# Second-key one-hots of the last quads on GpSimd, and the first v gathers issued between them

## The reference, cut to what matters

```
u_sel = u[expert]                      # 256 tokens x 128 chosen rows
v_sel = v[expert]
act = gelu(einsum('td,thkd->thk', x, u_sel))
out = einsum('thk,thkd->td', gate * act, v_sel)
h = layer_norm(ALPHA * h + out, ln2_g, ln2_b)
```

## Time and profile before

| | |
|---|---|
| median of 3 runs | 2725.31 us (2724.09 to 2729.93) |
| span of the profiled execution, first to last instruction | 2723.7 us |
| time around that span | not shown on its own; the lowest run is 0.4 us longer than the span, the median 1.6 us |
| TensorE busy | 2335.6 us, 86% |
| VectorE busy | 1951.1 us, 72% |
| GpSimd busy | 2045.3 us, 75% |
| ScalarE busy | 1283.7 us, 47% |
| TensorE's mean granted clock | 0.916 |

### The profile page before, as it was taken

How to read it: one execution, slowest core, us unless ns; L and a number is a source line. 1 busy time by engine, 2 the same in 40 slices (tenths; PEclk the granted TensorE clock), 3 DMA queues, 4 the chain that set the end, 5 groups by cost and what they waited for, 6 DMA issues and landing times. The chain is left out here.

```text
span 2723.7 us, 41417 instructions
## 1 busy us (share of the span) xinstructions
PE 2335.6 (86%) x13836; PEld 2071.9 (76%) x13836; DVE 1951.1 (72%) x2992; ACT 1283.7 (47%) x2249; POOL 2045.3 (75%) x1052
## 2 busy tenths in 40 slices
PE   7998999999999999999999876773334479999996
PEld 6997888888888888999988766772322368888885
DVE  4999752633514417456525999989998899999998
ACT  5435555455454455343433012327996844444442
POOL 4776888888888887778783566778788847777773
PEclk9999999999999999999999988885556589999998
DMA  6553465565555654554455999999999969999996
GB/s 218 171 162 113 170 179 176 192 187 187 185 187 185 185 186 161 173 198 166 148 187 186 413 391 384 378 422 417 379 416 384 395 219 384 385 365 374 380 371 256
DMA packets 232086, 722.75 MB, mean 265 GB/s; under 512 B 17388, under 2 KB 53796, under 8 KB 198816
## 3 DMA queue, kind: packets, MB, share of 16 engines
q1 hardware_dynamic: 168480, 355.69, 38.6%
q0 software_dynamic: 57344, 360.74, 33.1%
q10 hardware_dynamic: 6144, 4.81, 0.6%
HBM read 717.51 MB, written 3.67 MB: 265 GB/s over the span
## 5 line engine op out<-in xcount | busy, mean ns | idle before, releaser
L460 POOL TENSOR_TENSOR w_lo<-raw,w_hi 128x1024 fp32r<-128x1024 f32 x464 | 1131.2, 2456 | 293.0 <-ACT w_hi L1161 291.1
L1161 ACT CAST w_hi<-raw 128x1024 fp32r<-128x1024 f32 x464 | 483.6, 1050 | 634.7 <-PE bank L598 406.6
L596 PE MATMUL bank<-B,w_hi 128*128 128x512 f32 x1280 | 454.7, 400 | 11.3 <-DVE B L1746 7.0
L596 PE MATMUL bank<-A,w_hi 128*128 128x512 f32 x1280 | 451.2, 398 | 1.6 <-DVE A L1759 1.6
L598 PE MATMUL bank<-B,w_lo 128*128 128x256 f32 x1280 | 359.8, 281 | 0.0
L598 PE MATMUL bank<-A,w_lo 128*128 128x256 f32 x1280 | 358.4, 280 | 0.0
L1879 DVE TENSOR_TENSOR sq<-bank,T 128x256 f32<-128x256 f32 x128 | 54.1, 424 | 409.8 <-ACT T L1342 409.7
L601 PE MATMUL bank<-A,w_hi 128*128 128x256 f32 x1152 | 330.7, 287 | 6.7 <-DVE upad L1823 5.3
L550 POOL DMA_INDIRECT vrows<-in_peer_v,ering x192 | 265.3, 1382 | 87.6 <-DVE rest L2294 43.4
L602 PE MATMUL bank<-A,w_hi 128*128 128x256 f32 x1152 | 326.6, 283 | 0.0
L603 PE MATMUL bank<-A,w_lo 128*128 128x256 f32 x1152 | 326.5, 283 | 0.0
(11 more groups left out here) (348 smaller groups left out, 5187.4 us busy)
## 6 DMA issues: line engine op xcount, KB each, us to landing
raw<-in_mlp_w SPq DMA_DIRECT2D x128, 1024.0 KB, 5.2
v_raw<-in_peer_v SPq DMA_DIRECT2D x128, 672.0 KB
raw<-in_w_in SPq DMA_DIRECT2D x40, 1024.0 KB, 4.9
raw<-in_cc_w_in SPq DMA_DIRECT2D x64, 512.0 KB, 5.0
raw<-in_cc_w_out SPq DMA_DIRECT2D x16, 1024.0 KB, 5.0
raw<-in_w_out SPq DMA_DIRECT2D x16, 1024.0 KB, 5.0
raw<-in_peer_wq SPq DMA_DIRECT2D x8, 1024.0 KB, 11.2
wq_t<-in_peer_wq SPq DMA_DIRECT2D x2, 2048.0 KB, 24.4
```

The lines of the kernel that those rows point to most:

```text
L460: nc.gpsimd.tensor_tensor(w_lo[:, s % 4], raw[:, s // 2, 2 * (s % 2):2 * (s % 2) + 2, :], w_hi[:, s % 4].bitcast(F32), ALU.subtract).then_ ...
L596: nc.tensor.matmul(bank[m][:].rearrange("p (s t) -> p s t", s=2), wh, both[:, :, kt, :], start=(kt == 0), stop=False)
L1161: nc.scalar.copy(w_hi[:, s % 4], raw[:, s // 2, 2 * (s % 2):2 * (s % 2) + 2, :]).then_inc(hi_done, 1)
```

## The change

For 12 of the last 16 quads (q modulo 4 below 3: 48, 49, 50, 52, 53, 54, 56, 57, 58, 60, 61, 62) GpSimd makes the second key's one-hots, with four tensor_scalar instructions of 128 x 128 a quad, and raises a new semaphore `key_hot_ok`. VectorE makes for those only the four products, and for quads 51, 55, 59 and 63 all five instructions as before. GpSimd does its first two quads ahead of the wait for the last dot product, then the expert copy, and then in turns one of the six gathers and one quad, until the gathers are used up; the last four quads follow without gathers. Each quad waits on GpSimd for its buffer (`quad_ps`). TensorE waits for both semaphores. Loops over the last 16 quads on TensorE and VectorE become straight-line code.

```
+LAST_QUADS = range(EARLY_STEPS, TOK // 4)
+POOL_QUADS = [q for q in LAST_QUADS if q % 4 < 3]
+def key_hots(q):
+    return 4 * sum(p <= q for p in POOL_QUADS)
+def vector_hots(q):
+    return 13 * EARLY_STEPS + sum(4 + (p not in POOL_QUADS) for p in LAST_QUADS if p <= q)
@@ gpsimd
+            def key_hot(q):
+                pool.wait_ge(keyT_ok, 1)
+                pool.wait_ge(quad_ps, q + 1)
+                for i in range(4):
+                    nc.gpsimd.tensor_scalar(hot[:, q % 2, 1, i, :], cst[:, C_IOTA:C_IOTA + KEYS],
+                                            keyT[:, 1, 4 * (q - 32) + i:4 * (q - 32) + i + 1], None, ALU.is_equal
+                                            ).then_inc(key_hot_ok, 1)
             V_FIRST = NT * SLOTS // RING
+            for q in POOL_QUADS[:2]:
+                key_hot(q)
             pool.wait_ge(row_used, RING + NT * SLOTS)
             value_experts(0, 0, 0)
-            value_rows(V_FIRST, 0, 0, V_ROWS)
+            for n, q in enumerate(POOL_QUADS[2:]):
+                if n < V_ROWS:
+                    value_rows(V_FIRST, 0, n, 1)
+                key_hot(q)
@@ tensor
+            def quad(q, h):
+                pe.wait_ge(mat_ok, q + 1)
+                for i in range(4):
+                    last = nc.tensor.matmul(misc[2 + h][:, i * P:(i + 1) * P], hot[:, h, 1, i, :],
+                                            hot[:, h, 0, i, :], start=True, stop=True)
+                last.then_inc(quad_ps, 1)
+            def last_quads(first, end):
+                for q in range(first, end):
+                    pe.wait_ge(oh_ok, vector_hots(q))
+                    pe.wait_ge(key_hot_ok, key_hots(q))
+                    quad(q, q % 2)
-            quads(24, 1)
+            last_quads(48, 50)
             part_weights(3)
             pe.wait_ge(coefT_ok, 1 + PARTS)
-            quads(25, 7)
+            last_quads(50, 64)
@@ vector
-            def one_hots(r):
-                for h in range(2):
-                    q = 2 * r + (h + 32)
-                    dve.wait_ge(quad_ps, q + 1)
+            def one_hots(q):
+                h, first = q % 2, 4 * (q - 32)
+                dve.wait_ge(quad_ps, q + 1)
+                if q not in POOL_QUADS:
                     V.tensor_tensor(hot[:, h, 1], iota.unsqueeze(1).broadcast_to([P, 4, KEYS]),
...
+            for q in LAST_QUADS[:2]:
+                one_hots(q)
             part_coefficients(3)
+            for q in LAST_QUADS[2:8]:
+                one_hots(q)
             dve.wait_ge(coefT_ok, 1 + PARTS)
+            for q in LAST_QUADS[8:]:
+                one_hots(q)
```

More of the change, by code:

```diff
@@ L313, in build @@
             "keyT_ps", "keyT_ok", "coefT_ps", "coefT_ok", "oh_ok", "quad_ps", "mat_ok")
-        key_neg_ok = sem("key_neg_ok")
+        key_neg_ok, key_hot_ok = sems("key_neg_ok", "key_hot_ok")
         fq_ps, fq_ok, ln1_scaled = rbB_ok, n_out["rms1"], BT_in
@@ L1051, in quads @@
                     for h in range(2):
[L1052 to L1061, removed]
+                        pe.wait_ge(oh_ok, 13 * (2 * r + h) + 13)
+                        quad(2 * r + h, h)
+            def last_quads(first, end):
[3 more added lines that the diff above has]
+                    quad(q, q % 2)
             def row_turned(n):
@@ L2248, in gates_in_parts @@
                 dve.sem_inc(half_ok, 1)
-            def one_hots(r):
-                for h in range(2):
-                    q = 2 * r + (h + 32)
-                    dve.wait_ge(quad_ps, q + 1)
+            def one_hots(q):
+                h, first = q % 2, 4 * (q - 32)
+                dve.wait_ge(quad_ps, q + 1)
+                if q not in POOL_QUADS:
                     V.tensor_tensor(hot[:, h, 1], iota.unsqueeze(1).broadcast_to([P, 4, KEYS]),
[L2256 to L2262, removed]
+                                    keyT[:, 1, first:first + 4].unsqueeze(2).broadcast_to([P, 4, KEYS]), ALU.is_equal
+                                    ).then_inc(oh_ok, 1)
+                for i in range(4):
+                    V.tensor_scalar(hot[:, h, 0, i, :], iota, keyT[:, 0, first + i:first + i + 1],
+                                    coefT[:, 1, first + i:first + i + 1], ALU.is_equal, ALU.mult).then_inc(oh_ok, 1)
             def coefficients(t, n):
@@ L2345, in _ @@
             dve.wait_ge(coefT_ok, PARTS)
-            with dve.Fori(EARLY_STEPS // 2 - 16, EARLY_STEPS // 2 - 15) as r:
-                one_hots(r)
+            for q in LAST_QUADS[:2]:
+                one_hots(q)
             part_coefficients(3)
-            with dve.Fori(EARLY_STEPS // 2 - 15, EARLY_STEPS // 2 - 12) as r:
-                one_hots(r)
+            for q in LAST_QUADS[2:8]:
+                one_hots(q)
             dve.wait_ge(coefT_ok, 1 + PARTS)
-            with dve.Fori(EARLY_STEPS // 2 - 12, 16) as r:
-                one_hots(r)
+            for q in LAST_QUADS[8:]:
+                one_hots(q)
             dve.wait_ge(rest_ok, 1)
```

## The result

The changed kernel takes 2739.82 us in the median of six runs (2729.57 to 2745.70); six runs of the kernel before on the same chips took 2730.61 (2724.09 to 2733.79). The ratio is 1.005 with an interval of 1.0031 to 1.0068: slower by 9.2 us between the medians, and by 13.7 at the centre of the interval. The prediction was 2726.6 us, 1.3 later than before, with a range of 2721 to 2733. It was wrong: the time lies above the range. The range also ended 7.7 us above the 2725.3 from which it was reckoned, and the shift was 9.2.

What follows compares the result with a forecast made beforehand. VectorE paces the last quads before; after the change GpSimd is slowest from quad 52. With t = 0.36, 2206.9 + 32 t puts quad 63 at 2218.4, 1.3 us later: 2725.3 + 1.3 = 2726.6 us, range 2721 to 2733.

Steps and rivals of the forecast that it cites:

- The limit of what can be won: Quads 52 to 63: two-buffer round of 1.3 us a quad, plus quad 48's sooner start, allows at most 4.2 us.
- The price t: One GpSimd 128x128 tensor_scalar for the one-hots: taken as 0.36 us, 0.33 plus 0.03 for the port.
- The prediction's other estimate, 0.38: Same GpSimd tensor_scalar, from 1.8 cycles an element at 1.2 GHz: near 0.38 us, end 0.6 us later.
- The rest of the sum: GpSimd series from quad 52: one-hots, gathers 5.0, buffer wait 1.5, last steps 3.2; quad 63 starts at 2206.9 + 32 t.
- quad 62's own way: End of the GpSimd series: path through quad 62, claimed shorter than that through quad 61 while t is under 0.5.
- Before quad 50: First eight GpSimd one-hots beside VectorE's dots: 0.6 us delay against 0.61 saved, net 0; quad 50 at 2195.17 as before.
- signs that the prediction had named for being wrong: t under 0.3, one-hots of quads 48 and 49 unfinished when VectorE leaves the dots, or PEclk 0.5 in last quads.
- The fourth rival: Before quad 50: all 8 GpSimd instructions delay the dots in full, 4.4 us later, 2729.7 us; chance 0.07.
- The first (cheap instruction): GpSimd one-hots cost only 0.2 to 0.26 us each: 2721.1 to 2723.6 us; chance 0.18.
- The second (the lock at full length): Each GpSimd one-hot from 2197 waits out a VectorE product: t 0.585, 8.5 us later, 2733.8 us; chance 0.12.
- The third (the clock): TensorE half busy in last quads falls to 1.2 GHz: 2.1 us there, about 2 in dense, 2730.7 us; chance 0.11.

Runs made afterwards that it cites:

- both runs: Changed kernel with GpSimd copies for tensor_scalar: last dot product to first dense matmul 30.2 us; changed kernel with half the GpSimd one-hot instructions: 32.2 us.
- the run with the filler: Changed kernel plus four identity matmuls on TensorE ahead of each quad from 50 on: last dot product to first dense matmul 43.3 us, ratio 1.0014.
- first experiment: Kernel before plus 20 extra GpSimd instructions ahead of its first weight work: tensor_scalar 0.59 us each; last dot product to first dense matmul 31.5 us.

## Why the prediction was wrong, point by point

**The limit of what can be won** (4.2 us) was not contradicted: the best stretch was 2.2 us under the first profile of before.

**The price t is the step that failed.** The prediction took 0.36 us and bounded it from 0.2 to 0.55. Measured it is 0.605, and 0.59 by itself. The upper bound came from the line of GpSimd's two-input tensor_tensor (0.46, and 0.55 with waits), and the value from the thought that an input less should halve the slope of that line. The prediction's other estimate, 0.38, fails with it. The tensor_scalar is another operation with its own slope, 2.5 ns an element, above the 2.1 that I had read for two inputs. What does run at 0.8 ns is the copy. The Trainium skill, GPSIMD Engine Reference, "Engine selection", calls one-input instructions there roughly line rate; the copy fits that, the tensor_scalar does not, and the measurement decides.

**The rest of the sum.** The stretch by it is 22.1 + 32 t (2206.9, and 3.4 to the dense matmul, less 2188.18). At 0.28 us that gives 31.1 (measured 30.2), at 0.30 31.7 (32.2). That agreement is in part luck: in both runs GpSimd began quad 52 some 7.5 us after the last dot product, where the sum has 9.0, and then waited 2.6 and 3.0 us for buffers, where it has 1.5. At 0.605 quad 62's own way is the longer one, as the prediction said it would be from 0.5 on: 36 t in place of 32 t, 36 x 0.605 = 21.8, plus 5.0 and 1.5, then about 1.1 to quad 63 and 3.4 to the dense stage, from 9.0 after the last dot: 41.8. Measured 44.0. So of the 10.4 us between the sum as predicted (33.6 at 0.36) and the measurement the price makes 8.2. The gathers cost 1.2 to 1.3 each as said, and GpSimd began quad 52 9.2 us after the last dot product in place of 9.0. Of the 2.2 that are left, 1.7 are the two waits for a buffer, 3.15 in place of 1.5, and with TensorE at full clock they were 1.60; the others are 0.4 for one-hots beside VectorE's work (0.617 each) and the 0.2 at quad 52.

**Before quad 50** the net was right (quad 50 started 7.4 us after the last dot product, 7.0 before), but by another way. The dots were hardly delayed: the last ones took 2.28 to 2.36 us in place of 2.29. GpSimd paid instead, 14.9 us for eight: five beside the dots took 2.0 to 3.8 us each, and the last three, after them, 0.59. So it was 2.2 us behind when the dots were done. That is one of the signs that the prediction had named for being wrong; the clock, at 0.5 in some of the last quads, is another. The fourth rival is out.

**The rivals.** The first (cheap instruction) comes near with copies: 1.3 to 2.2 us off the stretch, where it said 1.7 to 4.2. The second (the lock at full length) took 0.585 for the instruction, by luck near the measured 0.605, and said 8.5 later where the stretch is 11.6 later; its reason was wrong, since the price is there with VectorE idle. Such a lock does hold VectorE's products for about the length of a two-input GpSimd instruction; beside the tensor_scalar their mean rose from 352 to 400 ns only. The third (the clock) did come: 0.69 in the stretch. Its price there was 0.7 to 1.7 us, not the 2.1 for the quads, and six slow matmuls at the start of the dense stage, not 2 us.

Whole runs differ by 9 to 14 us, around the 11.6 of the stretch. But the run with the filler, whose stretch is 10.9 longer than before, had a ratio of only 1.0014, 3.8 us, and 10.4 at the upper end of its interval. Where the scatter of whole runs comes from, and what hides there, stays open.

## What to carry to other kernels

Don't take an instruction's price from another operation of the same engine: it may have another slope, with fewer inputs too. Where it isn't in the trace, the upper bound has to be wide, or the instruction timed by itself first. Work handed to a second engine in a chain with two buffers needs a short time from buffer free to buffer full, not only a low load. When runs scatter by more than the effect, compare the length of the touched stretch between two fixed events in the profiles, and profile twice.

## What the runs showed of the hardware

- GpSimd tensor_scalar of 128 elements: 0.60 us with a scalar by pointer, 0.52 with a constant; 1.24 for 384; the copy of 128 takes 0.29 (first experiment).
- A GpSimd tensor_tensor of 1.05 us between VectorE tensor_scalar instructions held these up for about its length (12 in 6.97 us in place of 3.1); GpSimd copies and tensor_scalar did so little (mean of a product 352 ns alone, 488 beside the tensor_tensor, 400 beside the tensor_scalar, 360 beside copies).
- GpSimd tensor_scalar beside VectorE's two-input work at the end of the dot products: 2.0 to 3.8 us each (five of them), 0.59 after it, while the dots lost under 0.1 each.
